# Attention unrolled by pairs of heads: scores on two row halves, steps by branch from the widest query block to the narrowest

## The reference, cut to what matters

```python
# MLA: 8 heads, query and key 96 wide (64 + 32 rotary), value 64, dense causal
s = einsum('bqhd,bkhd->bhqk', q, k) * 96 ** -0.5
o_mla = einsum('bhqk,bkhd->bqhd', masked_softmax(s, kpos <= qpos), v)

# NSA: 8 heads of 64 in 2 kv groups, three branches with a relative bias each
s = einsum(q, k_cmp) * scale + bias      # c: 63 compressed keys
s = einsum(q, k_sel) * scale + bias      # s: top-16 of 16 blocks: all causal keys
s = einsum(q, kwin)  * scale + bias      # w: a window of 512 keys
out = g0 * o_cmp + g1 * o_slc + g2 * o_win   # sigmoid gates, per head and query
```

## Time and profile before

| | us |
|---|---|
| median of 3 runs | 4298.7 (4295.0 to 4320.8) |
| the profiled execution | 4301.8 |
| its span in the trace | 4300.0 |
| first load issue of the attention stage, from the span's start | 751.2 |
| its first matmul | 763.5 |
| its last store issue | 1706.5 |
| experts stage, first gather of rows | 2095.5 |

### The profile page before, as it was taken

How to read it: one execution, slowest core, us unless ns; L and a number is a source line. 1 busy time by engine, 2 the same in 40 slices (tenths; PEclk the granted TensorE clock), 3 DMA queues, 4 the chain that set the end, 5 groups by cost and what they waited for, 6 DMA issues and landing times. The chain is left out here.

```text
span 4300.0 us, 50598 instructions
## 1 busy us (share of the span) xinstructions
PE 3597.1 (84%) x16004; PEld 2660.0 (62%) x16005; DVE 1310.4 (30%) x3711; ACT 648.4 (15%) x1506; POOL 176.3 (4%) x187
## 2 busy tenths in 40 slices
PE   3447765899999998798499999999999999999970
PEld 1124445667666666465477776877778777777750
DVE  1114551443443343355222221222222222222213
ACT  0001110232333332132101000100011000100100
POOL 0000000000000000011000000000000000000000
PEclk7678885555566655897699999999999999999995
DMA  3222223211111011221566445764677655555716
GB/s 105 94 107 42 44 35 59 48 36 36 36 35 36 23 36 30 95 62 35 199 229 220 172 155 186 261 227 172 224 261 264 220 191 207 214 175 184 263 61 234
DMA packets 345115, 571.32 MB, mean 133 GB/s; under 512 B 123134, under 2 KB 150142, under 8 KB 343912
## 3 DMA queue, kind: packets, MB, share of 16 engines
q1 hardware_dynamic: 304984, 526.53, 36.7%
q0 software_dynamic: 21152, 38.50, 2.6%
q10 hardware_dynamic: 18832, 4.33, 0.5%
HBM read 531.15 MB, written 72.19 MB: 140 GB/s over the span
## 5 line engine op out<-in xcount | busy, mean ns | idle before, releaser
L1539 PE MATMUL ps<-xT_e,wg 128*128 128x128 f32 (+2 forms) x8192 | 1266.8, 318 | 71.1 <-DVE aT L1502 50.0
L1539 PEld LDWEIGHTS ps<-xT_e,wg 128*128 128x128 f32 x8192 | 1224.9, 200 | 126.3 <-DVE aT L1502 54.0
L1550 PE MATMUL ps<-wd,aT 128*128 128x512 f32 x1504 | 650.8, 592 | 0.0
L1550 PEld LDWEIGHTS ps<-wd,aT 128*128 128x128 f32 x1504 | 283.3, 190 | 344.4 <-issue 344.4
L1495 DVE TENSOR_SCALAR gg<-ps,bias 128x128 f32<-128x128 f32 (+2 forms) x256 | 101.4, 396 | 764.5 <-PE ps L1539 764.5
L696 PE MATMUL ps<-kn,qn 64*128 64x512 f32 (+3 forms) x384 | 270.8, 841 | 0.0
L711 PE MATMUL ps<-ident_t,sc 128*128 128x128 f32 x880 | 224.5, 393 | 44.8 <-ACT sc L754 29.4
L1508 DVE COPY ys_e<-ps 128x1024 f32<-128x1024 f32 x47 | 56.1, 1221 | 671.7 <-PE ps L1550 671.7
L754 ACT ACTIVATE sc<-sc,nm 128x640 f32<-128x640 f32 (+15 forms) x256 | 164.3, 642 | 638.2 <-DVE nm L790 638.2
L711 PEld LDWEIGHTS ps<-ident_t,sc 128*128 128x128 f32 x880 | 148.4, 197 | 170.1 <-issue 166.5
L728 PEld LDWEIGHTS ps<-vn,pT 128*128 128x128 f32 x1056 | 233.5, 325 | 0.0
(11 more groups left out here) (284 smaller groups left out, 2891.8 us busy)
## 6 DMA issues: line engine op xcount, KB each, us to landing
wg<-in_w_gate_up SPq DMA_DIRECT2D x128, 2048.0 KB, 7.8
wd<-in_w_down SPq DMA_DIRECT2D x128, 1024.0 KB, 4.9
yr<-d_ys SPq DMA_DIRECT2D x8, 2048.0 KB, 7.3
skew<-d_rev SPq DMA_DIRECT2D x18, 512.0 KB, 5.2
w_in<-in_w_in SPq DMA_DIRECT2D x1, 6880.0 KB
d_strip<-strip SPq DMA_DIRECT2D x9, 512.0 KB, 2.6
x_a<-in_x POOLq DMA_DIRECT2D x8, 512.0 KB, 7.5
kn<-d_kn SPq DMA_DIRECT2D x8, 512.0 KB
```

The source lines that it names most:

```text
L1539: mm = pe.matmul(ps[:, j % 2, half * PASS:half * PASS + w], wg[:, j // 2, k, c0:c0 + 255:2], xT[:, k, 0:w], start=(k == 0), stop=(k == KD ...
L1550: mm = pe.matmul(ps[:, 2 + 2 * b + h, :], aT[:, j, b * P:(b + 1) * P], wd[:, c, j % 2, h * 512:(h + 1) * 512], start=(j == 0), stop=(j == ...
```

## The change

The loop over heads becomes straight code over four pairs of heads. A unit is one pair, one branch, one query block; both heads go through each hand in turn. What changes in detail:
- The order of units within a pair is m, s, w, c, and in each branch from q = 7 down to q = 0. The pipeline of PE (`turn`, `values` of the unit before, `scores` two ahead) now runs on across branches and pairs.
- NSA queries, keys and compressed keys of the two heads lie on partitions 0 to 63 and 64 to 127 (both heads of a pair share a kv group, so the keys are loaded twice). The score matmuls of the heads alternate between these halves, in pieces of at most 512 columns, each head's into its own bank (`2 * (piece % 2) + h`).
- The row maximum is taken with negated sign: one instruction for each piece gives minus the scores and their minimum, the second piece starting from the first's; `exps` uses scale -1. The separate negation is gone.
- Transposes of head h go to bank 4 + h for both groups of four tiles; the second group follows `values` of the unit before. ACT copies head 0's, DVE head 1's.
- `finish` makes one reciprocal, one gate product and, in m and s, one final product for both heads; in w and c two final operations.
- All operands are held for two pairs. SP loads two pairs at the start, and later ones when the pair two before is done; outputs are stored once a pair.
- The gates are stored as rows of 24 values in `stage_project`, and loaded once; `sc` is set to zero by POOL instead of DVE and is twice as large.

```diff
-                        with nc.allow_non_contiguous_dma("12-byte gates"):
-                            sp.dma_start(e.d_gt[:, rows, :].rearrange("h p d -> p h d"), gt[b][:, :].rearrange("p (h d) -> p h d", d=3)).then_inc(s_st, 16)
+                        sp.dma_start(e.d_gt[rows, :], gt[b][:, :]).then_inc(s_st, 16)
...
-    STEPS = [(b, q) for b in "mcws" for q in range(NT)]
+    ORDER = [(b, q) for b in "mswc" for q in reversed(range(NT))]
+    PAIRS = HM // 2
+    NU = len(ORDER)
+    UNITS = [(hp, b, q) for hp in range(PAIRS) for b, q in ORDER]
...
+    def parts(u):
+        return (width(*UNITS[u][1:]) + 511) // 512
+
+    FIRST = [sum(parts(k) for k in range(u)) for u in range(len(UNITS) + 1)]
+    DEPTH = 4
...
+                    sp.dma_start(qn[:, k, :], e.d_qn_flat[2 * hp:2 * hp + 2].rearrange("h d n -> (h d) n")).then_inc(s_ln[k], 16)
+                    for h in range(2):
+                        half = slice(h * HD, (h + 1) * HD)
+                        sp.dma_start(kn[half, k, :, :], e.d_kn[:, g * HD:(g + 1) * HD, :].rearrange("w d n -> d w n")).then_inc(s_ln[k], 16)
+                        sp.dma_start(ck[half, k, :], e.d_ck[g]).then_inc(s_ln[k], 16)
+                        sp.dma_start(strip[:, k, h, :], e.d_strip[2 * hp + h]).then_inc(s_ln[k], 16)
+                        sp.dma_start(wstrip[:, k, h, :], e.d_wstrip[2 * hp + h]).then_inc(s_ln[k], 16)
+                        sp.dma_start(vn[:, k, h, :, :], e.d_vn[h][g].rearrange("(t p) d -> p t d", p=P)).then_inc(s_ln[k], 16)
...
                 load_mla(0)
-                with sp.Fori(0, HM - 1) as h:
-                    head(h, False)
+                load_nsa(0)
+                load_mla(1)
+                load_nsa(1)
+                for hp in range(PAIRS):
+                    if hp + 2 < PAIRS:
+                        load_mla(hp + 2)
+                        load_nsa(hp + 2)
+                    store(hp)
...
+                    for piece, c0, w in pieces(u):
+                        if piece >= 2:
+                            pe.wait_ge(s_m, 2 * (piece - 1))
+                        for h in range(2):
+                            half = slice(h * HD, (h + 1) * HD)
+                            out = ps[:, 2 * (piece % 2) + h, 0:w]
+                            cols = slice(lo + c0, lo + c0 + w)
+                            rows = slice(q * P, (q + 1) * P)
+                            if b == "m":
+                                mm = pe.matmul(out, qm[:, k, h, rows], km[:, k, h, cols], start=True, stop=True)
+                            elif b == "c":
+                                mm = pe.matmul(out, qn[half, k, rows], ck[half, k, 0:w], start=True, stop=True)
...
+                def turn(u, g):
+                    n = len(tiles(*UNITS[u][1:]))
+                    for h in range(2):
+                        pe.wait_ge(s_p, 2 * u + h + 1)
+                        if TURNS[u] + g:
+                            pe.wait_ge(s_cp[h], TURNS[u] + g)
+                        for i in range(4 * g, min(n, 4 * g + 4)):
+                            mm = pe.transpose(ps[:, 4 + h, (i % 4) * P:(i % 4 + 1) * P], sc[:, u % DEPTH, h, i * P:(i + 1) * P], ident[:, :])
+                        mm.then_inc(s_t[h], 1)
...
+                for u in range(len(UNITS)):
+                    turn(u, 0)
+                    if u:
+                        values(u - 1)
+                    if TURNS[u + 1] - TURNS[u] == 2:
+                        turn(u, 1)
+                    if u + 2 < len(UNITS):
+                        scores(u + 2)
...
+                def copies(u, g):
+                    for h in range(2):
+                        if by_scalar(h, g) and g < TURNS[u + 1] - TURNS[u]:
+                            dst, src = copy_probs(act, u, h, g)
+                            act.activation(dst, src, ACT.Copy).then_inc(s_cp[h], 1)
+
+                def exps(u):
+                    k, n = u % DEPTH, parts(u)
+                    w = width(*UNITS[u][1:])
+                    for h in range(2):
+                        act.wait_ge(s_m, 2 * (FIRST[u + 1] - 1) + h + 1)
+                        act.activation(sc[:, k, h, 0:w], sc[:, k, h, 0:w], ACT.Exp, bias=nm[:, k, h, n - 1:n], scale=-1.0,
...
+                        dve.tensor_tensor_reduce(sc[:, k, h, c0:c0 + w], ps[:, 2 * (piece % 2) + h, 0:w], bias_of(u, h, c0, w), -1.0,
+                                                 nm[:, k, h, c - 1:c] if c else 3.0e38, ALU.add, ALU.min, nm[:, k, h, c:c + 1]).then_inc(s_m, 1)
...
+                    if SEEN[(hp, "m" if b == "m" else "n", q)] == u:
+                        dve.tensor_tensor(y[:, hp % 2, q, :, :], O, bcast(co[:, k, :].unsqueeze(2), [P, 2, VD]), ALU.mult).then_inc(s_y, 1)
+                    else:
+                        dve.scalar_tensor_tensor(y[:, hp % 2, q, 0, :], O[:, 0, :], co[:, k, 0:1], y[:, hp % 2, q, 0, :], ALU.mult, ALU.add)
+                        dve.scalar_tensor_tensor(y[:, hp % 2, q, 1, :], O[:, 1, :], co[:, k, 1:2], y[:, hp % 2, q, 1, :], ALU.mult, ALU.add).then_inc(s_y, 1)
...
+                    if u + 1 < len(UNITS):
+                        peak(u + 1, 0)
+                    copies(u, 0)
+                    if u + 1 < len(UNITS):
+                        peak(u + 1, 1)
+                    if u:
+                        finish(u - 1)
+                    copies(u, 1)
+                finish(len(UNITS) - 1)
```

More of the change, by code:

```diff
@@ new lines, in stage_attend @@
+        s_lm, s_ln = [plain(f"t_load_mla{i}") for i in range(2)], [plain(f"t_load_nsa{i}") for i in range(2)]
+        s_ym, s_yn = [plain(f"t_ym_stored{i}") for i in range(2)], [plain(f"t_yn_stored{i}") for i in range(2)]
+        s_s, s_m, s_p, s_o, s_y, s_dch = (plain("t_" + n) for n in ("scores", "max", "probs", "out", "y", "dve_chain"))
+        s_t, s_cp = [plain(f"t_turned{h}") for h in range(2)], [plain(f"t_copied{h}") for h in range(2)]
+        N_LM, N_LN = 4, 12
+        dy = e.d_y.rearrange("(t p) n -> p t n", p=P)
@@ L634, in stage_attend, with pieces, by_scalar @@
+        def pieces(u):
+            full = width(*UNITS[u][1:])
+            return [(FIRST[u] + c // 512, c, min(512, full - c)) for c in range(0, full, 512)]
+        def by_scalar(h, g):
+            return h == 0
         with nc.Block() as block:
@@ L729, in values @@
-                        mm.then_inc(s_o, 1)
-                    scores(0)
-                    scores(1)
-                    for i in range(NS):
-                        turn(i)
-                        if i:
-                            values(i - 1)
-                        if i + 2 < NS:
-                            scores(i + 2)
-                    values(NS - 1)
+                                mm = pe.matmul(out, pT[0:w, u % 2, h, 0:P], cv[0:w, k, :], start=True, stop=True)
+                            elif b == "m":
+                                mm = pe.matmul(out, pT[:, u % 2, h, n * P:(n + 1) * P], vm[:, k, h, t, :], start=(n == 0), stop=(n == len(ts) - 1))
+                            else:
+                                mm = pe.matmul(out, pT[:, u % 2, h, n * P:(n + 1) * P], vn[:, k, "sw".index(b), t, :], start=(n == 0), stop=(n == len(ts) - 1))
@@ new lines, in _, with step, peak @@
+                n = [0]
+                def step(ins):
+                    ins.then_inc(s_dch, 1)
+                    n[0] += 1
+                    dve.wait_ge(s_dch, n[0])
+                def peak(u, c):
+                    k = u % DEPTH
+                    hp, b, q = UNITS[u]
+                    if b != "m" and c == 0:
+                        dve.wait_ge(s_ln[hp % 2], 16 * N_LN * (hp // 2 + 1))
+                    if c >= len(pieces(u)):
+                        return
+                    piece, c0, w = pieces(u)[c]
+                    for h in range(2):
+                        dve.wait_ge(s_s, 2 * piece + h + 1)
+                        if c:
+                            dve.wait_ge(s_m, 2 * (piece - 1) + h + 1)
+                        elif u >= DEPTH:
+                            dve.wait_ge(s_t[h], TURNS[u - DEPTH + 1])
+                        dve.tensor_tensor_reduce(sc[:, k, h, c0:c0 + w], ps[:, 2 * (piece % 2) + h, 0:w], bias_of(u, h, c0, w), -1.0,
+                                                 nm[:, k, h, c - 1:c] if c else 3.0e38, ALU.add, ALU.min, nm[:, k, h, c:c + 1]).then_inc(s_m, 1)
@@ new lines, in _ @@
+                dve.wait_ge(s_set, 1)
+                dve.wait_ge(s_c, 48)
+                peak(0, 0)
+                peak(0, 1)
+                for u in range(len(UNITS)):
+                    if u == 1:
+                        dve.wait_ge(s_gate, 16)
+                        step(dve.tensor_scalar(gates[:, 0, :, 0], gates[:, 0, :, 0], cvalid[:, 0:1], None, ALU.mult))
+                    if u + 1 < len(UNITS):
+                        peak(u + 1, 0)
+                    copies(u, 0)
+                    if u + 1 < len(UNITS):
+                        peak(u + 1, 1)
+                    if u:
```

(2 more changed lines are left out.)

274 lines of the change are left out of this document (105 added, 169 removed).

## The result

| | before | after |
|---|---|---|
| median of the runs, us | 4300.1 (4295.0 to 4320.8, 4 runs) | 3864.2 (3858.2 to 3866.0, 4 runs) |
| ratio, 95% interval | | 0.898 (0.895 to 0.901) |
| span of the profiled execution | 4300.0 | 3856.3 |
| first load issue of attention to its first matmul | 12.3 | 14.8 |
| first matmul to last store issue | 943.0 | 495.3 |

The kernel is faster by 10.2%. The whole gain lies in the attention stage; the stages ahead of it and behind it take what they took.

The account below looks back on a forecast made before the run. TensorE, mostly at its half clock level, was taken to bound attention. 572 - 40 + 19 = 551 us replaced 943.0 and loads of 19.5 replaced 12.3: 3915 of span, forecast as 3920 us, range 3865 to 4080.

Parts of the forecast that it names:

- Stage and bound: Attention stage: TensorE sets the time, mostly at half level (1.2 GHz); the untouched stages behind can only shift.
- Loads, +7: Before attention's first matmul: loads of two heads instead of one take 19.5 us in place of 12.3.
- Order, full level in m, s and w: Attention, order m, s, w, c, wide to narrow: full clock level, 0.55 us a tile instead of 1.14.
- Narrow steps at VectorE's pace: Attention, m, s and w: steps of one and two tiles bound by VectorE, 2.6 + 2.2 us in m.
- Overlap, a third: Scores of s and w on two row halves: four records take three places, about a third off, -40 us.
- c, lead-in and hand-offs: Attention: c 21 us a pair, entering m at half level +4, hand-offs at branch changes +19 in all.
- the lower end of c: Attention, c steps at their lower end: -31 us, would reach 3840 us; left out of the range.
- No overlap: Scores of s and w: full level, but the halves run one after the other, 3960 us; chance 0.15.
- Half level in s and w: Attention: s and w fall back to half level and stay, 4250 us without overlap, 4165 with; chance 0.15.
- Waits at each hand-off: Wide steps of m, s, w: each waits 1.18 us, 113 instead of 19 us, about 4015 us; chance 0.12.
- Code that arrives late: Unrolled attention stage, every engine's instruction stream: code arrives too late, 358 us of stops, 4280 us; chance 0.04.

Follow-up runs that it names:

- order alone: The kernel after with both heads' NSA queries on partitions 0 to 63, so nothing runs on two row halves: 3914.7 us, ratio 0.910.
- c second: The kernel after with both heads on the same rows and branches m, c, w, s, each from wide to narrow: 4052.7 us, ratio 0.940.
- neither: The kernel after with branches m, c, w, s, each narrow to wide, and both heads on the same rows: 4136.4 us, ratio 0.962.

## Why the prediction was off, point by point

**Stage and bound: right.** TensorE's half level in the attention stage was the price, and the gain lies there alone; the gate store costs nothing, the projection stage ends where it did (666.1 against 666.4 us).

**Loads, +7: too much.** 14.8 us against 19.5 forecast and 12.3 before (13.1 to 16.1 in the other kernels of pairs). I scaled the time with the bytes that the first matmul needs, 1.5 to 2.6 MB. But other loads share the queue, and the engines moved 199 GB/s x 12.3 us = 2.45 MB before and 207 x 14.8 = 3.07 after: 1.25 times the bytes in 1.2 times the time. -5 us.

**Order, full level in m, s and w: right in result, incomplete in reason.** 0.544 us a tile against 0.55, clock 1.00 in all three branches. But I gave it to the order alone. The runs show two causes of which either would do, and the order alone is only safe with pairs (0.986 in the old loop). Of the two parts of the order I named, "wide first" carries 25 to 84 us and "c last" 138 to 197, on the same rows in pairs. By that, what kept the level down in the earlier trace rows was probably above all that w and s were entered from c, and less that each branch began narrow; no run of the old loop tests the two apart.

**Narrow steps at VectorE's pace: wrong.** I priced the steps of one and two tiles in m, s and w at 15.3 us a pair (2.6 + 2.2, twice, and 3.0 + 2.7). The sum closes with PE's price in their place, 9 tiles x 1.10 = 9.9 us. PE's order lays the scores of the next branch's widest blocks (806.28, 809.41 us in the first pair) between them, and VectorE works ahead meanwhile. PE's waits for VectorE come to 2.1 us in the whole stretch (the rows below), and 65 us more on VectorE changed the stretch by 0.2 us. That is -5.4 us a pair, **-22**. VectorE's busy time is 312 us, not 353, without effect.

**Overlap, a third: too small.** The four records of the two heads take the place of two, not of three. I had each head's first or last record stand alone, three places for four records; the records start in pairs, 6 to 7 ns apart, as told below. 132 x 0.215 / 2 = 14.2 instead of 9.9 us a pair, **-17**. By the 2x of the Trainium skill (TensorEngine Tiling (Array Packing), Theoretical Speedup) the term was -59, and the trace agrees with that: 1.91 us became 1.06, 2.35 became 1.28. The halves bring no new price for changing over. A record of 512 columns takes 0.43 us at full level in m (1.72 / 4), so of the 1.06 us two places are 0.86 and 0.20 is left for going in and out; with both heads on the same rows it is 1.91 - 1.72 = 0.19. The same page of the Trainium skill (Key Properties) says that a change of tiling mode drains TensorE; 0.2 us at each group of 64-row scores, and none at m's with 96 rows, agrees with that in kind, but no run here shows that a drain is its cause.

**c, lead-in and hand-offs: too much together.** Forecast 21 + 4 + 19 / 4 = 29.8 us a pair. What is left of 123.2 after 93 wide tiles at 1.09 (101.4), the narrow ones (9.9) and the overlap (-14.2) is 26: 3.7 us a pair less, **-15** in all. The c steps took 13 us (875.00 to 887.05 and 893.24 to 894.14), not 21, which is -32 by itself; VectorE doesn't set their pace either, by the same 65 us. The first scores of the next m took 6.2 us at half level (887.05 to 893.24) for 8 x 0.43 = 3.4 at full, 2.8 more: the lead-in of 4 was about right. The hand-offs, 19 us, were too much: PE is idle for 12.9 us over the whole stretch, all causes included, and of that only 7.1 us in front of transposes that wait for ScalarE's copy. The rows of PE's waits for ScalarE's copy and for VectorE in the kernel after (us in total, times, longest):

```profile
PE ps L741 <- ACT pT L790: 7.1, 9, 1.1
...
PE ps L741 <- DVE pT L837: 1.5, 4, 0.4
PE ps L731 <- DVE nm L830: 0.6, 4, 0.2
```

The rest, some 7 us a pair, I had no term for: 0.2 us for going in and out of the scores in each of the 16 steps of s and w is 3 of it. What the other 4 are is not shown.

**Sum.** 551 - 22 - 17 - 15, and -4 for wide tiles at 1.09 in place of 1.10, is 493, as measured from turn to turn (4 x 123.2); from the first matmul to the last store it is 495.3. With 493 and with 14.8 for the loads the span comes to about 3853, measured 3856.3. The 26 us of a pair are what is left over, so that the sum closes is no proof of its parts. So the mechanism held and terms of the sum were mis-sized: the narrow steps at VectorE's pace, the overlap, the c steps and the loads, all to the same side. The added terms gave 3912 for the runs, and I rounded up to 3920, away from the result.

**Smaller slips.** The earlier trace rows has 5 and 6 tenths in the stage, not 5 to 7. The 4.48 us of the earlier trace rows lie behind the next head's first scores, not right behind the values. That 102 tiles at half level came to 116 us of a head's 118 was luck: it takes m's wide tiles at half, which the earlier trace rows shows at full, and leaves c out. And from 3920 to 4300 us it takes 85 stops of 4.48 us, not 87.

**The range.** Its low end was the sum with the full overlap, no hand-off and no extra load. I named the lower end of c (3840) and left it out, and had no lower end for the narrow steps at all: "bound by VectorE" was stated as a fact where no row of before shows two heads in a step. Both were unknown costs and belonged in the range. A row's own pace (one head, nothing beside it) was taken for a lower bound of a step that runs beside others.

**The rivals.** No overlap: refuted ("order alone" is that kernel, 3914.7 us; I had 3960). Half level in s and w: not in the kernel after, but real in three of four pairs without both of its causes (4136.4; I had 4165 to 4250). Waits at each hand-off: refuted by 12.9 us of idle. Code that arrives late: refuted for the unrolled stage, whose straight code costs nothing that shows (114 + 37 instruction packets, 91 + 56 before). But a late-code loss exists in a later stage, in a loop that the change only shifts. The kernel after escaped that loss of 55 us by luck, by where the loop happened to fall; the forecast had no term for it.

## What to carry to other kernels

Read the clock beside "busy" before counting instructions: a TensorE that is busy throughout can run at half level for most of a stage, and the remedy may be which steps follow which, or how the matmuls are laid on the rows. Try to put the work that drops the level (here c) directly ahead of work that raised it fast (here wide m), and to pair contractions of 64 on both row halves: here it nearly halved the time of those matmuls, and the level rose with it. When a part of a range rests on "this engine bounds that step", ask what runs beside it in the new order, and give the term two ends. And when a change in one stage costs time in another that nobody touched, look at waits for "issue" at the head of a loop and at the packets of the instruction queues before looking for data.

## What the runs showed of the hardware that I had not expected

**Records of two row halves start together.** In the first s step of the kernel after, the trace has the records of the two heads at 806.285 and 806.291, 806.818 and 806.825, 807.247 and 807.254, 807.676 and 807.683 us: always one of each head, 6 to 7 ns apart, and the second records of both heads only after the first of both. Eight records of 512 columns take four places of 0.43 us, with 0.1 us more behind the first and the last pair (the next transpose starts at 808.203), although the program issues both records of one head ahead of the other's. So matmuls on different row halves, into different banks, overlapped fully here, in float32.

**Half level without a gap.** In 64-row steps of single heads PE was busy for 22.00 of 22.00 us at 0.50, and the same steps held 1.00 in earlier heads. With both row halves in use the level rose within w, 11 us behind its first scores (834.5, 1.00 from 846 on, old order). Work on 64 rows alone can do it too, but later: two heads on the same rows regained the level 18 us into s with c second and once in "neither". The halves change two things at once, the rows in use and the share of the time that goes to scores, and no run separates them, so the cause stays open.

**A shifted loop can cost 55 us.** The experts loop has some 300 instructions on VectorE. Of five places in VectorE's stream one was bad: about five more packets of q14 in each pass ((194 - 37) / 31), 6 us of wait at its head. The Trainium skill (Runtime: NRT & Kernel Launch, Instruction fetch mechanics) says that an engine holds only two blocks of instructions, and that a branch to a place outside them has to be fetched first; the runs agree in kind, since only the place mattered, but none shows what lies where. The same section of the Trainium skill says that the cost of crossing into the next block in straight code is mostly hidden, and the unrolled stage agrees with that: PE is idle for 12.9 us in it, all causes included.
